# The even layer's two attentions: turned softmax weights in fp32 as the standing operand, division after the product, padded low pass of the keys

## What is computed

```python
# attention A: 8 query heads, 2 key/value heads, 64 wide
sc = jnp.einsum('bqkgd,bskd->bkgqs', qi, k) * scale
p  = jax.nn.softmax(sc, axis=-1)
o  = jnp.einsum('bkgqs,bskd->bqkgd', p, v)
# attention B: 8 heads, latent keys and values (64 + 32 rope wide), scale 96 ** -0.5
sc = (q_lat . c_kv + q_rope . k_rope) * scale
p  = softmax(sc);  o = (p . c_kv) . w_uv
y  = concatenate([oa * silu(ga), ob * silu(gb)]) @ w_out
```

## Time and profile before

| | |
|---|---|
| median of 3 runs | 3397.87 us (3397.43 to 3406.93) |
| profiled execution, its own time | 3408.66 us |
| its span, first to last instruction | 3406.9 us |
| TensorE busy, share of the span | 3176.5 us, 93% |
| VectorE / ScalarE busy | 1878.7 us, 55% / 1368.0 us, 40% |
| mean granted TensorE clock | 0.939 |
| first score matmul of A, of B | 2148.19 us, 2397.1 us |
| last value matmul of B | 2658.29 us |

### The profile page before, as it was taken

How to read it: one execution, slowest core, us unless ns; L and a number is a source line. 1 busy time by engine, 2 the same in 40 slices (tenths; PEclk the granted TensorE clock), 3 DMA queues, 4 the chain that set the end, 5 groups by cost and what they waited for, 6 DMA issues and landing times.

```text
span 3406.9 us, 39364 instructions
## 1 busy us (share of the span) xinstructions
PE 3176.5 (93%) x15816; PEld 2571.0 (75%) x15816; DVE 1878.7 (55%) x2435; ACT 1368.0 (40%) x2240; POOL 0.2 (0%) x4
## 2 busy tenths in 40 slices
PE   8999989789999989999999799999999889999987
PEld 6777768577898778888887577677888668877766
DVE  6552678753354344443444535789889543246753
ACT  4321545432253211111113334678878424246741
POOL 0000000000000000000000000000000000000000
PEclk9999977789999989999999899899999989989988
DMA  4113200311311222322221211100011121211031
GB/s 141 44 50 105 67 25 1 112 37 56 90 30 57 72 78 84 90 85 74 81 84 46 90 50 53 41 1 10 10 36 59 62 81 50 78 38 44 11 99 62
DMA packets 228115, 202.84 MB, mean 60 GB/s; under 512 B 8992, under 2 KB 202656, under 8 KB 227424
## 3 DMA queue, kind: packets, MB, share of 16 engines
q1 hardware_dynamic: 224352, 187.49, 17.9%
q10 hardware_dynamic: 3584, 12.85, 1.1%
HBM read 167.54 MB, written 30.41 MB: 58 GB/s over the span
## 4 chain that ended last, share of the span: by engine, by line
PE 85%; DVE 8%; ACT 4%; issue 2%; DMA 1%; SPq 0%; ACTq 0%; DVEq 0%
PE P L298 55%; PE P L267 5%; PE P L2058 5%; PE P L270 3%; PE P L272 2%; PE P L271 2%; PE P L2072 2%; PE P L2071 1%; PE P L2583 1%; PE P L2578 1%; PE P L398 1%; PE P L1346 1%; PE P L2580 1%; PE P L2582 1%; DVE T L1701 1%
## 5 line engine op out<-in xcount | busy, mean ns | idle before, releaser
L254 DVE TENSOR_TENSOR wl<-wf,wh 128x1024 fp32r<-128x1024 f32 (+4 forms) x239 | 251.7, 1053 | 1046.5 <-ACT wh L246 1046.3
L246 ACT ACTIVATE wh<-wf 128x1024 fp32r<-128x1024 f32 (+4 forms) x239 | 220.1, 921 | 1180.1 <-PE P L298 1071.3
L298 PE MATMUL P<-AQ,wh 128*128 128x512 f32 x1920 | 522.7, 394 | 16.5 <-DVE AQ L1314 10.4
L298 PE MATMUL P<-XH,wh 128*128 128x512 f32 (+1 forms) x1376 | 445.7, 406 | 74.7 <-DVE XL L1212 22.9
L298 PEld LDWEIGHTS P<-AQ,wh 128*128 128x128 f32 x1920 | 364.6, 190 | 96.5 <-issue 15.1
L298 PE MATMUL P<-XL,wh 128*128 128x512 f32 (+1 forms) x1376 | 435.8, 399 | 0.0
L298 PE MATMUL P<-XH,wl 128*128 128x512 f32 (+1 forms) x1376 | 435.2, 398 | 0.0
L298 PEld LDWEIGHTS P<-XH,wh 128*128 128x128 f32 (+1 forms) x1376 | 260.2, 192 | 153.9 <-issue 79.8
L298 PEld LDWEIGHTS P<-XL,wh 128*128 128x128 f32 (+1 forms) x1376 | 263.9, 192 | 59.8
L298 PEld LDWEIGHTS P<-XH,wl 128*128 128x128 f32 (+1 forms) x1376 | 263.4, 191 | 59.5
L298 PE MATMUL P<-AQ,wl 128*128 128x512 f32 x960 | 298.0, 392 | 0.0
(11 more groups left out here) (419 smaller groups left out, 5339.6 us busy)
## 6 DMA issues: line engine op xcount, KB each, us to landing
AW<-ada_w SPq DMA_DIRECT2D x48, 512.0 KB, 3.7
wf<-w_gate_up SPq DMA_DIRECT2D x44, 512.0 KB, 4.9
wf<-w_in SPq DMA_DIRECT2D x28, 512.0 KB, 3.8
scratch_g<-T ACTq DMA_DIRECT2D x24, 512.0 KB, 3.3
scratch_h<-H SPq DMA_DIRECT2D x24, 512.0 KB, 5.6
H<-scratch_h SPq DMA_DIRECT2D x24, 512.0 KB, 8.0
wf<-odd_w_in SPq DMA_DIRECT2D x20, 512.0 KB, 3.7
wf<-even_w_in SPq DMA_DIRECT2D x17, 512.0 KB, 3.8
```

The source lines that it names most:

```text
L246: e.activation(self.sb["wh"][i % 2][:, 0:m], self.sb["wf"][i % 2][:, 0:m], ACT.Copy).then_inc(*self.s.w_hi.up(i))
L254: e.tensor_tensor(l, f, h.bitcast(F32), ALU.subtract).then_inc(*self.s.w_lo.up(i))
L298: ins = e.matmul(self.P[slot][0:m, t:t1], w, x[:, k, t:t1], start=first and k == 0, stop=last and k == kb - 1)
```

## The change

The softmax weights are no longer divided by their sum before they are turned, and no longer split. After turning, ScalarE copies one half and VectorE the other half of a block as plain fp32 (tile PT). TensorE multiplies with the turned weights as the standing operand (128 keys x 128 queries) and the values, now plain fp32, moving (64 columns): eight fp32 matmuls for each block. The product comes out with queries on the partitions, so VectorE divides it there by the sums (`tensor_scalar` with a column of reciprocals) into tile OT, for two blocks at every odd position. Two heads make a block of 128 features; TensorE turns it back in two jobs of four transposes ("ot", 16 in all), and ScalarE copies each into O. The second score pass of A now moves a key tile that is padded with zeros to 128 rows; VectorE writes four zero halves once. VectorE's low parts of the values (one of 128x1024, eight of 128x512) are gone. Some tiles move in SBUF.

```diff
@@ dve_rotary_end
-                kh, kl = self.sb["KH2"][q], self.sb["KL2"][q]
+                kh = self.sb["KH2"][q]
                 e.wait_ge(*s.hi.to((name, q)))
-                e.tensor_tensor(kl[a, :], x[a, :], kh[a, :].bitcast(F32), ALU.subtract).then_inc(*s.lo.up())
-                e.tensor_tensor(kl[o, :], x[a, :], kh[a, :].bitcast(F32),
-                                ALU.subtract).then_inc(*s.lo.up((name, q)))
+                for p in range(2):
+
+                    kl, half, rest = self.sb["KL2"][p][q], slice(64 * p, 64 * p + 64), slice(64 - 64 * p, 128 - 64 * p)
+                    e.memset(kl[rest, :].bitcast(F32), 0.0).then_inc(*s.dve.up())
+                    e.tensor_tensor(kl[half, :], x[a, :], kh[a, :].bitcast(F32),
+                                    ALU.subtract).then_inc(*s.lo.up((name, q) if p else None))
@@ beside, operands, output
+        if n < 56 and n % 16 in (2, 4) and n > 15:
+            return "ot", n // 16 - 1, n % 16 // 4
...
+        if nxt % 2 and nxt > 0 and i in ((0, 4) if nxt == 3 else (2, 4)):
+            return "ot", (h - 2) // 2, i // 4
...
-            return [(sb["QS"][h], sb["KH2"][kv]), (sb["QS"][h][a, :], sb["KL2"][kv][a, :])], sb["VA"][:, :, kv, :]
+            return [(sb["QS"][h], sb["KH2"][kv]), (sb["QS"][h], sb["KL2"][h % 2][kv])], sb["VA"][:, :, kv, :]
...
+    def output(self, n):
+
+        c = 64 * (n // 8 % 2)
+        at = 512 * (n // 2 % 2) + 64 * (n % 2)
+        return self.P[3][:, at:at + 64], self.sb["OT"][n // 16 % 2][:, n % 8, c:c + 64]
@@ pe_attention
-                    e.wait_ge(*s.lo.to(("pt", n - 1, d)))
+                    e.wait_ge(*(s.dve if d else s.act).to(("pt", n - 1, d)))
...
-                e.wait_ge(*(s.act if d else s.dve).to(("sc", n)))
+                if d == 0:
+                    e.wait_ge(*s.act.to(("exp", n)))
...
+        def values(n):
+            u, v, o = n // 2 % 2, self.operands(n)[1], self.output(n)[0]
+            if n % 2 == 0:
                 wait(free[u])
...
+            for k in range(8):
+                ins = e.matmul(o, self.sb["PT"][n % 2][:, k, :], v[:, k, :], start=k == 0, stop=k == 7)
+            ins.then_inc(*s.mm.up(("pv", n)))
+            free[u] = [(s.dve, ("os", n))]
...
+            if kind == "ot":
+                block, t = job[1:]
+                last = 16 * block + 11 + 4 * t
+                e.wait_ge(*s.dve.to(("os", last)))
+                for k in range(4):
+                    ins = self.turn(e, o[:, 128 * k:128 * k + 128], self.sb["OT"][block % 2][:, 4 * t + k, :])
@@ act_attention
-                for d in range(2):
-                    e.wait_ge(*s.mm.to(("t", at, d)))
-                    if at > 3:
-                        e.wait_ge(*s.mm.to(("pv", at // 2 - 2)))
-                    e.activation(self.probs("PTH", at, d), self.turned(d), ACT.Copy).then_inc(*s.hi.up(("pt", at, d)))
-            at = n - 2
-            if 0 <= at < 128:
-                c = self.px(at)[:, 512:1024]
-                e.wait_ge(*s.dve.to(("inv", at)))
-                e.activation(c, c, ACT.Copy, scale=sb["WST"][at % 4][:, 2:3]).then_inc(*s.act.up(("sc", at)))
+                e.wait_ge(*s.mm.to(("t", at, 0)))
+                if at > 1:
+                    e.wait_ge(*s.mm.to(("pv", at - 2)))
+                e.activation(sb["PT"][at % 2][:, 0:4, :], self.turned(0), ACT.Copy).then_inc(*s.act.up(("pt", at, 0)))
@@ dve_attention
-                for d in range(2):
-                    self.dve_low(e, ("pt", at, d), self.probs("PTL", at, d), self.turned(d), self.probs("PTH", at, d))
...
-                e.tensor_scalar(a, a, sb["WST"][at % 4][:, 2:3], None, ALU.mult).then_inc(*s.dve.up(("sc", at)))
+                e.wait_ge(*s.mm.to(("t", at, 1)))
+                if at > 1:
+                    e.wait_ge(*s.mm.to(("pv", at - 2)))
+                e.tensor_copy(sb["PT"][at % 2][:, 4:8, :], self.turned(1)).then_inc(*s.dve.up(("pt", at, 1)))
...
+            for at in (n - 5, n - 4) if n % 2 and 5 <= n < 132 else ():
+                src, out = self.output(at)
+                e.wait_ge(*s.mm.to(("pv", n - 4)))
+                e.wait_ge(*s.dve.to(("inv", at)))
+                if at > 31 and at % 16 == 0:
+                    e.wait_ge(*s.mm.to(("ot", at // 16 - 2, 1)))
+                e.tensor_scalar(out, src, sb["WST"][at % 4][:, 2:3], None, ALU.mult).then_inc(*s.dve.up(("os", at)))
```

More of the change, by code:

```diff
@@ L1953, in dve_even @@
             if task == "va":
-                behind = self.dve_turn_values
+                behind = None
             elif task == "ck roots":
@@ L2006, in bank @@
     def bank(self, n):
-        return (n - 7) // 2 % 2
+        return 1 - n // 2 % 2
     def px(self, n):
@@ L2059, in scores @@
             ins.then_inc(*s.mm.up(("s", n)))
[L2061 to L2064, removed]
+        def values(n):
+            u, v, o = n // 2 % 2, self.operands(n)[1], self.output(n)[0]
+            if n % 2 == 0:
                 wait(free[u])
[L2066 to L2077, removed]
+            e.wait_ge(*s.act.to(("pt", n, 0)))
+            e.wait_ge(*s.dve.to(("pt", n, 1)))
+            if n % 32 == 0 and n >= 64:
+                e.wait_ge(*s.act.to(("VB", (n - 64) // 32, 3)))
+            for k in range(8):
+                ins = e.matmul(o, self.sb["PT"][n % 2][:, k, :], v[:, k, :], start=k == 0, stop=k == 7)
+            ins.then_inc(*s.mm.up(("pv", n)))
+            free[u] = [(s.dve, ("os", n))]
         def slab(name, g):
@@ L2086, in beside @@
             o = self.pv(u)
-            if kind in ("rope", "v", "q", "k"):
+            if kind in ("rope", "v", "q", "k", "ot"):
                 wait(free[u])
+            if kind == "ot":
[4 more added lines that the diff above has]
+                    ins = self.turn(e, o[:, 128 * k:128 * k + 128], self.sb["OT"][block % 2][:, 4 * t + k, :])
+                ins.then_inc(*s.mm.up(job))
+                free[u] = [(s.act, job)]
             if kind == "rope":
@@ L2106, in beside @@
                 ins.then_inc(*s.mm.up(("bank", "v", g, part)))
-                free[u] = [(s.lo, job)]
+                free[u] = [(s.act, ("VB", g, part))]
             elif kind == "q":
@@ L2135, in pe_attention @@
                 beside(n, job)
-            at, part = (n - 4, 0) if n % 2 else (n - 5, 1)
-            if 0 <= at < 128:
-                values(at, part)
-        self.emptied = {0: [(s.act, ("exp", 126))], 1: [(s.act, ("exp", 127))], 2: [(s.lo, ("pt", 127, 1))],
-                        3: [(s.dve, ("o", 63))]}
+            if 0 <= n - 4 < 128:
+                values(n - 4)
+        self.emptied = {0: [(s.act, ("exp", 126))], 1: [(s.act, ("exp", 127))], 2: [(s.dve, ("pt", 127, 1))],
+                        3: [(s.dve, ("os", 127)), (s.act, ("ot", 7, 1))]}
     def pair_free(self, h):
@@ L2169, in beside @@
                 e.wait_ge(*s.mm.to(("bank", "v", g, part)))
-                e.activation(sb["VB"][g][:, 2 * part:2 * part + 2, :, 0:64], src, ACT.Copy).then_inc(*s.hi.up(job))
+                e.activation(sb["VB"][g][:, 2 * part:2 * part + 2, :, :], src, ACT.Copy).then_inc(*s.act.up(("VB", g, part)))
+            elif kind == "ot":
+                block, t = job[1:]
+                e.wait_ge(*s.mm.to(job))
+                e.activation(sb["O"][:, block, 512 * t:512 * t + 512], o, ACT.Copy).then_inc(*s.act.up(job))
             elif kind == "q":
@@ L2262, in beside @@
                 self.dve_low(e, job, sb["RQL"][:, :], x, sb["RQH"][:, :])
[L2263 to L2267, removed]
             elif kind == "q":
@@ L2885, in places @@
     sb["KH2"] = [put(f"KH2{i}", "A", 32 * K + 4 * K * i, [128, S], F32R) for i in range(2)]
-    sb["KL2"] = [put(f"KL2{i}", "A", 40 * K + 4 * K * i, [128, S], F32R) for i in range(2)]
-    sb["VA"] = put("VA", "A", 48 * K, [128, 8, 2, 128], F32R)
+    sb["KL2"] = [[put(f"KL2{i}", "A", 40 * K + 4 * K * i, [128, S], F32R) for i in range(2)],
+                 [put("KL3", "A", 52 * K, [128, S], F32R), put("KL4", "H", 28 * K, [128, S], F32R)]]
+    sb["VA"] = put("VA", "A", 48 * K, [128, 8, 2, 64], F32)
     sb["AXIAL"] = put("AXIAL", "A", 56 * K, [128, 2, S], F32)
```

57 lines of the change are left out of this document (16 added, 41 removed).

## The result

The changed kernel takes 3439.56 us (median of 4 runs, 3436.83 to 3442.02), the kernel before beside it 3399.89 us (4 runs, 3397.43 to 3406.93). The ratio is 1.0113, with a 95% interval of 1.0094 to 1.0132: slower by 39.7 us, or 32 to 45 by the interval. The profiled execution took 3442.01 us, its span 3440.1.

A forecast was written before the change was run, and what follows sets the result against it. TensorE was taken to pace the attentions. Terms 2 + 51 + 7 - 13 - 5 - 2 gave +40 us on the profiled 3408.66 us (3449); adjusted to the median, 3440 us was predicted, range 3412 to 3490.

The forecast's parts named there:

- Values: Value matmuls on TensorE: sixteen load-priced records, 1.74 us a position; +0.73 in A, +0.80 in B (+51 us over B).
- Second pass: A's score passes on TensorE: with one height, four take 0.99 instead of 1.69 us, -0.70 a position.
- Turning the output back: 16 jobs of four transposes on TensorE's path, 0.11 us each: +7 us.
- Waits: TensorE's waits in A, B and the drain: nearly all 13.2 us go, at least 6; turning needs only the exponential.
- The divisions: VectorE's divisions of the output: waits behind them stay hidden, with at most 0.3 us at a rope's end.
- a sign of being wrong: In the attentions: TensorE waiting for the divisions before it fills a bank of P[3] would show the prediction wrong.
- Clock: Half-clock spells after long waits: -5 us in A's profiled execution, under 2 in B; the median might gain nothing.
- The rival that would prolong it to n = 25: Start of A: clock stays low until the first rope job, some 20 positions at 7 us, 3500 us; 14%.
- Streaming alone sets the price: Value matmuls: a fp32 record costs only what moves, 0.06 us; -57 us, 3341 us; 5%.
- The moving part not hidden: Value matmuls: moving columns add 0.06 us to each of 16 records at 124 positions, +119, 3560 us; 4%.
- Drain: End of the attentions: loses VectorE work, gains a turn and a copy; -2 us, bounds -4 and +2.

The follow-up runs named there:

- eight records: Changed kernel with turned weights and values rounded to fp32r, one record instead of two per value matmul: 3338.83 us, ratio 0.9807.
- without the scaling: Kernel before without scaling the weights by the reciprocal of their sums, no output division, turns waiting for the exponential alone: 3390.52 us, ratio 0.9962.
- The pass alone: Kernel before with A's second score pass on 128 rows: 3374.57 us; conversely, changed kernel with it back on 64 rows: 3490.41 us.

## Why the prediction was right

The forecast was 3440 us, slower, with a range of 3412 to 3490; 3439.56 was measured. The direction, the place of the loss and its mechanism were right. That the number fits within half a microsecond is luck: the changed kernel's own runs lie between 3436.83 and 3442.02, the kernel before moved from 3397.87 to 3399.89 with one more run, and on the profiled executions, where the sum was made, +33.35 us came of the +40. Terms that were off by up to 9 us partly cancelled. Point by point:

**Values.** Predicted 16 x 0.109 = 1.74 us, measured 1.73 in A and in B. The load-bound reading of the earlier trace rows was confirmed three times: by 32 columns costing what 64 cost, by eight records costing 0.81, and by records with 64 standing columns costing 0.060. In B the +0.80 came: 4.00 against 3.21. This is nearly the whole loss.

**Second pass.** Predicted -0.70 a position, measured -0.75 (in the kernel before, without other bounds) and -0.77 (in the changed one). Slightly mis-sized for one reason: a position has four open loads, and the fourth, between the last 64-row pass and the values, lies partly in the values (1.84 against 1.73), where I counted only the score passes. The same load made me read 1.015 for the old values in A, where they cost 0.93. The two errors cancel: +0.73 - 0.70 = +0.03 was forecast and 3.54 - 3.495 = +0.045 measured.

**Turning the output back.** A position with such a job takes 3.98 instead of 3.54 in A and 4.45 instead of 4.01 in B: 0.44, and 16 of them 7.0, as forecast.

**Waits.** Forecast was that 13.2 us of them nearly vanish because the turn needs only the exponential. In the trace of the changed kernel 1.6 and 1.3 us are left beyond the first positions, so the size was right, but the reason was half of it: without the scaling 5.8 us stayed. The 3.2 for a bank behind line 2306 of that kernel shows that VectorE's remaining work mattered; in the changed kernel that work is smaller: two low parts of 0.68 and the scaling gone, one copy of 0.69 and a division of 0.28 new. That this is what removed the bank's wait in B wasn't tried by itself.

**The divisions.** I gave their waits at most 0.3 us at a rope's end; 1.65 came there (timeline of the changed kernel, last column the idle time before):

```profile
2271.91 1.23 DVE L1314 TENSOR_TENSOR RQL<-T,RQH 128x1024 fp32r<-128x1024 f32 x1 [1.12 <-ACT RQH L2168]
...
2273.05 0.47 DVE L2306 TENSOR_SCALAR OT<-P,WST 128x64 f32<-128x64 f32 x2
...
2273.57 0.66 PE L267 MATMUL P<-consts,OT 128*128 128x128 f32 x4 [1.65 <-DVE OT L2306]
```

VectorE makes the rope's sum, waits 1.12 us for ScalarE's high part, makes the low part, and only then divides; the job "ot" at n = 34 is the first one behind it. By the program's order it isn't the job's input that is late: this was complete with block 27, divided at n = 31. The job writes into the bank of P[3] that holds the products of blocks 28 and 29, and these are the two divisions at 2273.05, made at n = 33 behind the rope's end. So TensorE waits for divisions before it fills a bank of P[3], which the prediction named as a sign of being wrong: on this term it was, by 1.35 us. A stretch of 3.4 us at clock 0.55 follows. I had looked at what the divisions hold up in the following position, and not at who needs their bank soon.

**Clock.** This is the term that was wrong in its place. I gave -5 us to the profiled execution for a spell of half clock behind the longest wait of A, and none to the median. The spell there did shrink, from 10.2 us to 3.4. But the one that went is the long one at A's start: its first eight positions take 22.5 us instead of 31.7, -9.2, nearly all of A's -9.5, and the sum had nothing for it. The rival that would prolong it to n = 25 did not occur: 1.00 from the first score to 2274.8 us. It names a rule of the Trainium skill, TensorE: Matmul & The Clock Gate, Part 4: PE-mode transpose, that full clock does not engage for transposes; with transposes in every position this trace shows 1.00 nearly throughout the attentions. In the profiles this spell, 20.5 us long, is there in the kernel before and in the one without the scaling (64-row passes and the old values); with 128-row passes, fp32 values, or both, none at that place is longer than 6.8 us. Each is one execution, so what holds the clock up there, and how often it would have fallen, stays open.

**Streaming alone sets the price.** This rival, by the passes that the Trainium skill counts for true FP32 (FP8 and Floating Point Precision, TensorE Precision Notes), fell: by passes and columns 32 columns should have been cheaper than 64, and were not. The moving part not hidden fell with it.

**Drain.** -2 forecast, -0.5 measured.

The changes are not additive. The pass alone gives -25 on the kernel before, and -51 on the changed one, because VectorE, with ScalarE close behind, binds in the one and not in the other; the values and what comes with them cost 3439.56 - 3374.57 = 65 us on top of the pass.

## What to carry to other kernels

Before a moving operand is made the standing one, count weight loads: when only some 64 columns move past each 128x128 block, the load is the whole price, and plain fp32 pays it twice. Where matmuls of 128 and 64 rows alternate, see in the trace whether the loads start only with their own pass; if so, padding the short ones to the full height closes them, and one of them shows in what follows the last one. Passes of 96 rows beside 128 needed no padding here. Before taking the gain of such an edit for certain, see how near the next engines are: here it gave 25 us instead of 45 to 51, and in a plain position a third of its value, until their work was moved away.

## What was unexpected in the hardware

GpSimd's scaling of 128x512 fp32 in SBUF took 1.57 us and of 128x1024 2.85, where VectorE takes 0.48 and ScalarE 0.72 for 512; while GpSimd ran, VectorE's own rose to 0.72, ScalarE's and VectorE's reads from PSUM did not move (0.68 for its low parts either way). A change between 128 and 64 rows costs about 0.19 us, in both directions: passes stand 0.42 us apart instead of 0.23, while a change between 128 and 96 rows costs nothing that shows. In plain fp32 sixteen records of 128x128 weights took 1.70 us with 1 and with 32 moving columns, and 1.73 with 64; half as wide a standing operand (fp32r) brought a record from 0.11 to 0.060 us.
